# A fused two-block transformer layer on one core: a second norm taken from sums, and another order inside the gate tiles

## The reference, cut to what matters

```python
# first block: mixer output -> residual -> norm -> feed-forward
y = sigmoid(gate_a) * a + sigmoid(gate_b) * cb
y = y @ w_mix_o                                   # the mixing projection
x = x + gt_m * rms_norm(y, g_post_mix)            # first norm
h = rms_norm(x, g_pre_ffn) * (1.0 + sc_f) + sh_f  # second norm
y = conv_ffn(h, w_up, w_dw, b_dw, w_down)
...
# second block, twice (l = a, b): side inputs
gate = sigmoid(rms_norm(h, ple_norm_g[i]) @ ple_w_gate[i])
h = h + (p[i] @ ple_w[i]) * gate
```

## Time and profile before

| what | us |
|---|---|
| three runs: lowest, median, highest | 1547.03, 1551.8, 1555.54 |
| the profiled execution | 1543.95 |
| its span in the trace | 1542.2 |
| PE busy | 1439.8 (93%) |
| DVE busy | 964.7 (63%) |
| ACT busy | 729.6 (47%) |
| POOL busy | 234.2 (15%) |

### The profile page before, as it was taken

How to read it: one execution, slowest core, us unless ns; L and a number is a source line. 1 busy time by engine, 2 the same in 40 slices (tenths; PEclk the granted TensorE clock), 3 DMA queues, 4 the chain that set the end, 5 groups by cost and what they waited for, 6 DMA issues and landing times. The chain is left out here.

```text
span 1542.2 us, 19717 instructions
## 1 busy us (share of the span) xinstructions
PE 1439.8 (93%) x6826; PEld 1142.9 (74%) x6826; DVE 964.7 (63%) x1512; ACT 729.6 (47%) x1249; POOL 234.2 (15%) x224
## 2 busy tenths in 40 slices
PE   5899899979978999999999999998998999999996
PEld 3688776768746888887887787777776778888775
DVE  5568887467665556565223757985564568888454
ACT  4425554553334445454113436775443446666342
POOL 3104633231110000000002000111120012222111
PEclk8899999989998999999999999999999999999998
DMA  9623234236511322223232332112222210000321
GB/s 385 222 95 96 82 132 130 93 109 205 194 53 55 104 86 94 96 83 108 96 95 68 103 109 62 61 50 96 82 82 82 96 55 28 28 28 28 116 90 55
DMA packets 39881, 151.65 MB, mean 98 GB/s; under 512 B 4784, under 2 KB 4928, under 8 KB 39040
## 3 DMA queue, kind: packets, MB, share of 16 engines
q1 hardware_dynamic: 29664, 105.92, 20.8%
q0 software_dynamic: 10144, 44.76, 8.0%
HBM read 144.37 MB, written 6.29 MB: 98 GB/s over the span
## 5 line engine op out<-in xcount | busy, mean ns | idle before, releaser
L639 PE MATMUL ps<-a_hi,w_hi 128*128 128x512 f32 x880 | 363.5, 413 | 25.6 <-ACTq L1382 11.8
L640 PE MATMUL ps<-a_lo,w_hi 128*128 128x512 f32 x880 | 351.5, 399 | 0.0
L641 PE MATMUL ps<-a_hi,w_lo 128*128 128x512 f32 x880 | 351.5, 399 | 0.0
L1566 DVE TENSOR_TENSOR w_lo<-w_raw,w_hi 128x1024 fp32r<-128x1024 f32 x126 | 166.2, 1319 | 128.1 <-ACT w_hi L1098 127.5
L639 PEld LDWEIGHTS ps<-a_hi,w_hi 128*128 128x128 f32 x880 | 167.9, 191 | 71.2 <-ACTq L1382 12.7
L641 PEld LDWEIGHTS ps<-a_hi,w_lo 128*128 128x128 f32 x880 | 167.7, 191 | 40.7
L640 PEld LDWEIGHTS ps<-a_lo,w_hi 128*128 128x128 f32 x880 | 168.3, 191 | 35.6 <-issue 0.5
L1098 ACT ACTIVATE w_hi<-w_raw 128x1024 fp32r<-128x1024 f32 x138 | 144.7, 1049 | 71.9 <-PE ps L641 54.8
L562 POOL TENSOR_TENSOR sq<-sq 128x512 f32<-128x512 f32 x36 | 46.6, 1294 | 569.0 <-ACT sq L1113 569.0
L639 PE MATMUL ps<-b_hi,w_hi 128*128 128x512 f32 x240 | 98.3, 410 | 5.5 <-DVE b_lo L1985 5.5
L641 PE MATMUL ps<-b_hi,w_lo 128*128 128x512 f32 x240 | 95.0, 396 | 0.0
(11 more groups left out here) (319 smaller groups left out, 2987.4 us busy)
## 6 DMA issues: line engine op xcount, KB each, us to landing
w_raw<-in_w SPq DMA_DIRECT2D x198, 512.0 KB, 3.5
ada_a<-in_ada POOLq DMA_DIRECT2D x16, 512.0 KB, 7.7
ada_g<-in_ada POOLq DMA_DIRECT2D x16, 512.0 KB, 3.8
ada_b<-in_ada POOLq DMA_DIRECT2D x16, 512.0 KB, 4.1
x_resid<-in_x POOLq DMA_DIRECT2D x2, 2048.0 KB, 11.8
pl_store<-pl_out POOLq DMA_DIRECT2D x2, 2048.0 KB, 8.7
pl<-pl_store POOLq DMA_DIRECT2D x2, 2048.0 KB, 9.9
alibi<-in_alibi POOLq DMA_DIRECT2D x16, 192.0 KB, 2.7
```

What stands on the lines that cost most here:

```text
L639: pe.matmul(o, w[0], r[0], start=start, stop=False, skip_group_check=skip)
L640: pe.matmul(o, w[0], r[1], start=False, stop=False, skip_group_check=skip)
L641: return pe.matmul(o, w[1], r[0], start=False, stop=stop, skip_group_check=skip)
L1566: dve.tensor_tensor(w_lo[:, n % SLOTS, :], raw, hi, ALU.subtract).then_inc(w_lo_done, 1)
```

## The change

**Second norm from sums.** With y' = g_post * y and r = the first reciprocal root, the new x is x + r y', so its sum of squares is S0 + r S3 + r r S2, where S0 sums x*x, S3 sums 2 x y' and S2 sums y'*y'. ACT squares each finished mix tile straight from PSUM, writes `y_f` already multiplied by the gain, and squares that too; it also squares the eight tiles of x. POOL adds up three sets of squares, 19 adds in the place of 6. DVE no longer copies to `y_f`; it forms the products 2 x y' and adds them in a PSUM bank (`cross_product`). PE makes four totals behind the projection, DVE combines them in four passes (`x_sum`), and ACT takes Ln and Exp. x itself is updated in the same DVE loop that makes the normed input. The last modulation group moves behind the sums.

**The first four up tiles** run together, k by k (`together`, which a_q now uses as well), and the loop is one turn shorter. The split of chunk up + 3 moves ahead of the loop, so the loop of ACT and DVE splits chunks one further on: the second split of a pair now waits for the second tile of that pair, ahead of both copies.

**Gate stages.** DVE does the low part of tile k - 1 between the scaling of tile k and its product with the side input, and the weight split at the end of a tile. ACT splits behind the sigmoid and squares x behind the next high part.

```diff
+            def add_gated_square(k):
+                if 1 <= k <= KT - 2:
+                    pool.wait_ge(s2_ready, k + 1)
+                    if k >= 2:
+                        pool.wait_ge(s2_used, k - 1)
+                    pool.tensor_tensor(s2[:, 0, :], s2[:, 0, :], s2[:, 1, :], ALU.add).then_inc(s2_used, 1)
+            def add_input_square(k):
+                pool.wait_ge(s0_ready, k + 1)
+                if k >= 2:
+                    pool.wait_ge(s0_used, k - 1)
+                pool.tensor_tensor(s0[:, 0, :], s0[:, 0, :], s0[:, k, :], ALU.add).then_inc(s0_used, 1)
+            for k in range(KT - 1):
                 add_square("mix", k)
+                add_gated_square(k)
+                for n in ((), (), (), (1,), (2, 3), (4, 5), (6, 7))[k]:
+                    add_input_square(n)
...
+            def residual_sums():
+                def total(at, src, start=True, stop=True):
+                    return pe.matmul(ps[:, at, :], ones[:, :], src, start=start, stop=stop, skip_group_check=True)
+                q = squares[0]
+                begin_event()
+                pe.wait_ge(sq_used, q + KT - 2)
+                total(STAT_BANK, sq[:, 0, :], stop=False).then_inc(sq_used, 1)
+                pe.wait_ge(s2_used, KT - 2)
+                total(S2_BANK, s2[:, 0, :], stop=False)
+                pe.wait_ge(sq_ready, q + KT)
+                total(STAT_BANK, sq[:, 1, :], start=False).then_inc(sq_used, 1)
+                pe.wait_ge(s2_ready, KT)
+                total(S2_BANK, s2[:, 1, :], start=False).then_inc(s2_sum, 1)
+                pe.wait_ge(s3_ready, KT - 1)
+                total(S3_BANK, s3[:, 0, :]).then_inc(s3_sum, 1)
+                pe.wait_ge(mod_ready, 5)
+                pe.wait_ge(s0_used, KT - 1)
+                total(MOD_BANK, s0[:, 0, :]).then_inc(s0_sum, 1)
+                squares[0] += KT
+            def together(name, src, ready, between=None):
+                def block(j, k):
+                    pe.wait_ge(ready, k + 1)
+                    w = weights(CH[name] + j)
+                    return mm3(ps[:, (LT[name] + j) % LIN, :], cols(w, P * k), (src[0][:, k, :], src[1][:, k, :]), k == 0, k == KT - 1, skip=True)
+                for j in range(LIN):
+                    free_bank(LT[name] + j)
+                for k in range(KT - 2):
+                    for j in range(LIN):
+                        block(j, k)
+                for j in range(LIN):
+                    block(j, KT - 2)
+                    block(j, KT - 1).then_inc(lin_done, 1)
+                    if between is not None:
+                        between(j)
+            residual_sums()
+            pe.wait_ge(x_sum_ready, 1)
             mod_group(5, acc_b)
-            added_squares("mix")
-            for k in range(KT):
-                square_sum(k, KT)
-
-            with pe.Fori(0, FT // 2) as i:
+            together("up", A, R["h2"])
...
-                        n = CH["up"] + k + WEIGHT_LEAD
+                        n = CH["up"] + k + LIN
                         act.wait_ge(w_land[n % RAW], i * 32 + 16 * (n // RAW + 1))
-                        act.wait_ge(lin_done, i * 4 + (LT["up"] + k))
+                        act.wait_ge(lin_done, i * 4 + (LT["up"] + k + 1))
                         act.activation(w_hi[:, n % SLOTS, :], w_raw[:, n % RAW, :], ACT.Copy).then_inc(w_hi_done, 1)
...
             for k in range(KT):
                 split(CH["mix"] + k + WEIGHT_LEAD)
-                square(y_f[:, k, :], R["y_f"], k + 1, k)
+                src = ps[:, (LT["mix"] + k) % LIN, :]
+                square(src, lin_done, LT["mix"] + k + 1, k)
+                act.wait_ge(gains, 2)
+                act.activation(y_f[:, k, :], src, ACT.Copy, scale=gvec[:, KT + k:KT + k + 1]).then_inc(R["y_f"], 1)
+                act.wait_ge(R["y_f"], k + 1)
+                if k >= 2:
+                    act.wait_ge(s2_used, k - 1)
+                act.activation(s2[:, min(k, 1), :], y_f[:, k, :], ACT.Square).then_inc(s2_ready, 1)
+                if 3 <= k < 7:
+                    act.wait_ge(x_in, 32)
+                    for n in (2 * k - 6, 2 * k - 5):
+                        act.activation(s0[:, n, :], x[:, n, :], ACT.Square).then_inc(s0_ready, 1)
             rsqrt(D)
-            for k in range(KT):
-                square(x[:, k, :], R["x_mix"], k + 1)
-            rsqrt(D)
-            act.wait_ge(gains, 4)
+            split(CH["up"] + WEIGHT_LEAD)
+            act.wait_ge(x_sum_ready, 1)
+            act.activation(rs[:, rss[0] % 3, :], x_sum[:, :], ACT.Ln, bias=EPS, scale=1.0 / D).then_inc(x_sum_ln, 1)
+            act.wait_ge(x_sum_ln, 1)
+            act.activation(rs[:, rss[0] % 3, :], rs[:, rss[0] % 3, :], ACT.Exp, scale=-0.5).then_inc(rs_ready, 1)
+            rss[0] += 1
...
-                    split(CH[l + "_gate"] + k + WEIGHT_LEAD)
                     act.wait_ge(R["gt"], KT * i + k + 1)
                     act.activation(gs2[:, k % 2, :], gs2[:, k % 2, :], ACT.Sigmoid).then_inc(R["gsig"], 1)
+                    split(CH[l + "_gate"] + k + WEIGHT_LEAD)
                     if k == KT - 1:
                         ln_exp_set()
                     if nxt is not None:
-                        scaled_input(nxt, "norm_b", k, R["x_ple"], KT * i + k + 1, k)
-                    else:
-                        square(x[:, k, :], R["x_ple"], KT * i + k + 1, k)
+                        act.wait_ge(R["x_ple"], KT * i + k + 1)
+                        act.activation(nxt[:, k, :], x[:, k, :], ACT.Identity, scale=v("norm_b", k)).then_inc(hi_done, 1)
+                    square(x[:, k, :], R["x_ple"], KT * i + k + 1, k)
...
+            def cross_product(n):
+                dve.wait_ge(x_in, 32)
+                dve.wait_ge(R["y_f"], n + 1)
+                src = y_f[:, n, :], 2.0, x[:, n, :], ALU.mult, ALU.mult
+                if n == 0:
+                    step(dve.scalar_tensor_tensor(ps[:, S3_BANK, :], *src))
+                    return
+                step(dve.scalar_tensor_tensor(s3[:, 1, :], *src))
+                dst = ps[:, S3_BANK, :] if n < KT - 1 else s3[:, 0, :]
+                dve.tensor_tensor(dst, ps[:, S3_BANK, :], s3[:, 1, :], ALU.add).then_inc(s3_ready, 1)
+                dve.wait_ge(s3_ready, n)
             for k in range(KT):
                 split(CH["mix"] + k + WEIGHT_LEAD)
                 for _ in range((2, *[1] * (KT - 2), 0)[k]):
                     mod_unit()
-                dve.tensor_copy(y_f[:, k, :], bank(LT["mix"] + k)).then_inc(R["y_f"], 1)
+                if k == 0:
+                    dve.wait_ge(mod_ready, 4)
+                    gain(2, "g_pre_ffn", 4, 1.0)
+                for n in ((), (), (0,), (1, 2), (3, 4), (5,), (6,), (7,))[k]:
+                    cross_product(n)
+            def scaled_y(y, k, gain_=None):
+                if gain_ is None:
+                    dve.tensor_tensor(y[:, k, :], y[:, k, :], r, ALU.mult).then_inc(dve_step, 1)
+                else:
+                    at_k = KT * gain_ + k
+                    dve.scalar_tensor_tensor(y[:, k, :], y[:, k, :], gvec[:, at_k:at_k + 1], r, ALU.mult, ALU.mult).then_inc(dve_step, 1)
+                steps[0] += 1
+            r = wait_rs()
+            dve.wait_ge(s2_sum, 1)
+            step(dve.tensor_tensor(x_sum[:, :], ps[:, S2_BANK, :], r, ALU.mult))
+            dve.wait_ge(s3_sum, 1)
+            step(dve.tensor_tensor(x_sum[:, :], ps[:, S3_BANK, :], x_sum[:, :], ALU.add))
+            step(dve.tensor_tensor(x_sum[:, :], x_sum[:, :], r, ALU.mult))
+            dve.wait_ge(s0_sum, 1)
+            dve.tensor_tensor(x_sum[:, :], ps[:, MOD_BANK, :], x_sum[:, :], ALU.add).then_inc(x_sum_ready, 1)
+            def new_input(k):
+                scaled_y(y_f, k)
+                dve.wait_ge(dve_step, steps[0])
+                step(dve.tensor_tensor(x[:, k, :], x[:, k, :], y_f[:, k, :], ALU.add))
+            new_input(0)
+            r2 = wait_rs()
+            dve.wait_ge(gains, 3)
+            for k in range(KT):
+                if k >= 2:
+                    dve.wait_ge(R["h2"], k - 1)
+                slot = tmp_slot()
+                dve.scalar_tensor_tensor(slot, x[:, k, :], gvec[:, 2 * KT + k:2 * KT + k + 1], r2, ALU.mult, ALU.mult).then_inc(tmp_w, 1)
+                if k + 1 < KT:
+                    new_input(k + 1)
+                his[0] += 1
+                dve.wait_ge(hi_done, his[0])
+                dve.scalar_tensor_tensor(a_lo[:, k, :], slot, mod[:, 3 * KT + k:3 * KT + k + 1], a_hi[:, k, :].bitcast(F32),
+                                         ALU.add, ALU.subtract).then_inc(R["h2"], 1)
+                if k == 0:
+                    split(CH["up"] + WEIGHT_LEAD)
...
-                    split(CH[l + "_gate"] + k + WEIGHT_LEAD)
                     g = gs2[:, k % 2, :]
                     dve.tensor_tensor(g, bank(LT[l + "_gate"] + k), r, ALU.mult).then_inc(R["gt"], 1)
+                    if nxt is not None and k:
```

(6 more changed lines are left out.)

71 lines of the change are left out of this document (21 added, 50 removed).

## The result

| | before | after |
|---|---|---|
| runs timed together: median (lowest to highest), us | 1549.41 (1544.61 to 1555.54), 4 | 1527.75 (1526.77 to 1529.5), 4 |
| the profiled execution, us | 1543.95 | 1527.43 |
| its span, us | 1542.2 | 1525.6 |
| PE busy, us | 1439.8 (93%) | 1433.8 (94%) |

The ratio of the times is 0.9859, interval 0.982 to 0.9898. The two profiled executions lie 16.5 us apart where the sum of the prediction said 15.7. So the terms of the sum nearly held, and what failed is the last step, from the profiled execution to the median. The experiments go after both.

A forecast was written before the change was run, and what follows sets the result against it. PE, busy 93% of the span, was taken as the bound, so time is its work plus gaps. Terms -12.9 + 4.1 - 6.9 = -15.7 from 1543.95 gave 1528.2, plus 7.9 carried over 1536.1; range 1528 to 1546.

The forecast's parts named there:

- Net norm part: From mix through the first four up tiles: done at 481.2 instead of 494.1, net gain 12.9 us.
- Meetings: Between mix and up, POOL's adds and DVE's passes take turns, 1.10 us per add, delaying the y sum by 3.8 us.
- Rival A: Meetings of POOL and DVE cost nothing and the clock holds from up to down: 1530 us, chance 0.17.
- rival B: Full spacing of POOL's adds (+3.7) and only 4.5 us gained in the gate tiles: 1542 us, chance 0.18.
- Pause ahead of down: From up to down, PE's pause grows by 2.2 us and a lower clock behind it costs 1.9: 4.1 lost.
- Gate tiles: Layer a's gate tiles: DVE follows PE and b_c's wait shrinks to 0.4 us: 6.9 gained.
- Rivals C and D: C: first four up tiles at half clock, 1552, chance 0.05. D: ACT's up-loop round exceeds two tiles, 1563, chance 0.05.
- The step that failed: From profiled execution to median: 7.9 us carried over from the kernel before, turning 1528.2 into 1536.1.

The follow-up runs named there:

- no_x_adds: The changed kernel without POOL's seven adds of x squares, so the sum S0 is incomplete; 1527.04 us in one run.
- relief: The changed kernel with two POOL adds of x squares fewer, which PE totals itself, and three others one tile later; 1527.73 us, ratio 0.9878.
- copies_first: The changed kernel with ACT's second split of a pair in the up loop moved behind both copies; 1525.72 us, ratio 0.9866.
- copies_second: The same program as copies_first, run a second time beside the unedited changed kernel; 1524.74 us.
- after_third: The changed kernel unedited, timed again beside the kernel before; 1530.05 us, ratio 0.9882.
- again: The changed kernel unedited, timed again beside the kernel before in the same rounds; 1529.44 us, ratio 0.9879.

## Why the prediction was right and where it was wrong

**Net norm part, right: -12.9 predicted.** In the table it is -14.35 + 1.02 = -13.3 up to the last up matmul. Most of the 1.0 is what the prediction counted when it let the last input tile, not PE, end the first four tiles: PE's wait of 0.48 at 476.39 and its slow step behind it lose 0.75. The rest is a longer start at the half level, seven steps of 0.43 where before had five.

**Meetings, right in kind, 0.4 too dear.** 3.8 predicted, 3.4 by no_x_adds; with the 0.4 that the unhindered way was shorter, that is why the first low part came 0.7 us ahead of the prediction. Rival A, no cost at all, falls. Of rival B, the full 1.44 for each add and a gain of 4.5 in the gate tiles, nothing is seen. relief adds what the prediction had not: behind POOL, DVE's own queue is late too.

**Pause ahead of down, right.** 2.2 more predicted for the pause and 1.97 measured; 1.9 for the clock and 1.54 measured as 434.02 - 432.48. The clock's part can be read at its own place too: the first 30 steps of down take 8.61 us in after (709.05 to 717.66) and 7.08 in before (719.45 to 726.53), 1.53 apart. copies_first and copies_second, with 1.54 of pause and 7.08 for these steps, show that both hang on the one split ahead of the copies.

**Gate tiles, right.** -6.9 predicted, -6.78 measured, with the wait of 0.4 and full clock behind it.

**Rivals C and D.** The first four up tiles ran at the half level only at their start (0.77 and 0.63 long, then 0.40), and behind 476.7 no step of PE in the up projection is longer than 0.3 us. Both fall.

**The step that failed.** "The median of the runs shown is 1551.8, 7.9 higher, and I carry the difference over: 1536.1." The sum itself, 1528.2 against the profiled execution, came out at 1527.43; that it is off by only 0.8 is partly luck, since the terms were off by 0.9 together and after_third, the same program, took 1530.08. The 7.9 were taken from three runs that spread over 8.5 us, as if they were a property of the kernel; over 55 runs the difference is 2.7. With 2.7 the forecast would have been 1530.9, against the 1529.0 that 15 runs gave. The range inherited the fault: its low end was rival A's 1530, already carried over, less 2. Without anything carried over the same rival gives 1522.5, and that is where the low end belonged, since nothing said whether the profiled execution or the median of three was the better guess of where before stands.

## What to carry to other kernels

A sum of waits read from one profiled execution says how far two profiled executions lie apart; before it is put on top of a median of three runs, look at how widely those three spread, and let the range hold both the carried and the uncarried time. Cut the spans at a few instructions that both kernels have, count from such a cut and not from the start of the span, and read each term at its own place. And when an engine's row is made shorter, work out who is second and where the moved work lands, since here 2.95 us less of POOL bought 0.45.

## What was not expected of the hardware

The granted clock differs between executions of one program, behind identical waits. In copies_first PE's totals behind waits of 1.90 and 1.02 us ran partly at 1.2 GHz (1.91 us for a pair), in after, again, after_third and copies_second at full speed (1.02), worth 1.4 us. The restart behind the wait of 1.18 us near 844 is the same: at the half level in copies_first and relief, at full speed in the other eleven traces, whose waits there are 1.17 to 1.60.

Behind the 3.50 us pause ahead of down it is otherwise. All six traces that have it lost clock, and the first 30 steps of down lost 1.56 to 1.62 us in each (against 30 steps of 0.233); in the seven with 1.54 us of pause they lost 0.08. Only the place moves a little: in relief the first steps were full ones, and the lower stretch came in 710 to 715 (0.68).

```profile
708.00:710.00 2.00, 1.25 (x5) 1.10 (x6) 1.59 (x3) 0.65 (x2) 0.00 (x0) 0.96 0.37 127
710.00:715.00 5.00, 5.00 (x16) 3.90 (x16) 2.26 (x4) 1.26 (x2) 0.00 (x0) 0.68 0.14 57
```

no_x_adds lost the 1.56 there as well, and yet its column to b_c is only 0.15 us longer than before's, since less was lost later: the granted clock in 1030 to 1060 was 1.00, where after and before had 0.94. So this term of the clock is steady when it is read right behind its pause, and the column of 430 us, which sums up several such places, is not enough to prove or refute it from one trace of each kernel.
